# Head of a decoder block kernel: input rows loaded first and handled chunk by chunk, first weight unit in pieces, identity built on the chip, sixteen unread transposes while the rows load

## The chip, the cores and the metric

The kernel runs on one core of a Trainium2 chip. The metric is the device time of one execution in microseconds (us); lower is better. The core has TensorE (PE, with its weight loads PEld), VectorE (DVE), ScalarE (ACT), GpSimd (POOL) and SyncE (SP), which run apart from each other and meet at semaphores.

## The reference

One decoder block on 512 tokens of width 1024, in float32, cut to what matters here:

```python
def rms_norm(x, g):
    y = x * rsqrt(mean(x * x, axis=-1, keepdims=True) + 1e-5)
    return y * g

h = rms_norm(x, norm_mix_g)
proj = h @ w_in                                  # 1024 x 3584: rq, rk, rv, rg, aq, ak, av
rq, rk, aq, ak = (rotary(t, pos) for t in (rq, rk, aq, ak))
ret = silu(rg) * head_group_norm(retention_chunkwise(rq, rk, rv))
att = dilated_mixture(aq, ak, av)
x = x + concat([ret, att], -1) @ w_out
x = x + moe_ffn(rms_norm(x, norm_ffn_g), ...)    # top 4 of 32 experts, each 1024 -> 2x1024 -> 1024
out = rms_norm(x, norm_final_g)
```

## The kernel before

Tokens are cut into four chunks of 128 rows (`NC`). Weights come in units of 1 MB, 128 partitions by 2048 columns, through four buffers `raw`. A float32 product is made of three products in a faster format: ScalarE rounds a unit or an input to its high part (`hi(n)` writes `whi`, `hT_hi` for the input), VectorE subtracts to get the low part (`lo(n)` writes `wlo`, `hT_lo`), and TensorE adds high x high, low x high and high x low. A unit that goes by one of `hi(n)` and `lo(n)` is read by four calls of `unit_chunk`, one for each chunk, with 12 matmuls of 512 columns each.

The head of the kernel, up to the projection's first products, is what the change rewrites. SyncE loads unit 0, then the four row chunks of x, then units 1 to 3. ScalarE's queue loads the gain of the norm and the identity matrix (64 KB of constants), later the other constants and the cosines (`mix`). TensorE waits for the identity, turns the gain, transposes the rows for feature blocks j = 0 to 6 over all four chunks, and ScalarE and VectorE split a feature block of all 512 tokens at a time with the gain as a scale. The row factor 1/rms is not in these inputs: ScalarE squares the four chunks (L790) after `hi(1)`, takes a root (L793), VectorE makes `row_rms` (L1126 to L1130) and multiplies the cosines and sines with it (L1151).

The projection is a list of steps b = 0, 1, 2, ... (`project(b)`): unit n = b // 4, chunk c = b % 4; units 0 and 1 make the first group (AQ), 2 and 3 the next. All engines have the same order of steps written out by hand, and each of them works strictly in its own order. VectorE's order around the head is:

```python
            for b in range(8 * NG):
                n, c = divmod(b, NC)
                gi, u = divmod(n, 2)
                if c == 0 and not 20 <= b < 44:
                    lo(n + 2)
...
                if u == 1 and GROUPS[gi] in (AQ, AK, RQ, RK):
                    rotate(n_rot, b)
```

So `lo(2)`, `lo(3)` and then `rotate(0)` stand behind the scaling of the cosines. TensorE transposes the first rotated rows (`transpose_rot(0)`, L1658) right after step b = 6, and step 7 stands behind it.

Of the kernel before, what the change touches and what calls it, by code (L numbers as in the profile page):

```python
# [25 lines left out]
P = 128  # L26
# [39 lines left out]
LAST_BANK = [0, 2, 6, 4]  # L66

# [88 lines left out]
def build(nc, x, norm_mix_g, w_in, w_out, norm_ffn_g, w_router, b_router,  # L156
# [161 lines left out]
    def sem(name):  # L318
        return nc.alloc_semaphore(name)
# [3 lines left out]
    hi_done, lo_done = sem("hi_done"), sem("lo_done")  # L323
    used = sem("units_used")
# [3 lines left out]
    slots_in, pairs_tok, ones_s = sem("slots_in"), sem("pair_tokens"), sem("ones_ready")  # L328
    has_s, pair_tr, idx_first_s = sem("slots_of_expert"), sem("first_rows_product"), sem("first_rows_index")
    table_cleared, entry_tok, entry_s, entry_out, tab_in = (sem("table_cleared"), sem("entry_tokens"), sem("entries_ready"),  # L330
# [45 lines left out]
    f_sum, f_sq, f_var, f_root, f_out, stored = (sem("final_sum"), sem("final_squares"), sem("final_variance"),  # L376
                                         sem("final_root"), sem("final_rows"), sem("outputs_stored"))
# [23 lines left out]
    HEAD_BANK = [4, 5, 6, 7, 1, 2, 3, 4]  # L401
# [37 lines left out]
    def raw_unit(r, rows):  # L439
        return raw_slot(r).rearrange("p (k c) -> p k c", k=rows)  # L440
# [15 lines left out]
    with block as block:  # L456
        @block.sync
        def _(sp):
# [26 lines left out]
            load(0, 0, mixer_source(0), KU)  # L485
            for c in range(NC):
                sp.dma_start(x1[:, c, :], x[0, c * P:(c + 1) * P, :]).then_inc(x_in[c], 16)
# [61 lines left out]
        def _(pl):  # L549
# [20 lines left out]

            pl.wait_ge(a_prob, NC * H)
# [6 lines left out]
            with nc.allow_non_contiguous_dma(reason="rows of 128 bytes, and 1024 gains onto partitions"):  # L578
# [6 lines left out]
            pl.wait_ge(cst_in, 32)  # L585
# [5 lines left out]
                                  cst[:, C_ROW:C_ROW + NC].unsqueeze(2).to_broadcast([P, NC, TOPK])).then_inc(entry_tok, 1)  # L591
            nc.gpsimd.tensor_copy(tab[:, E, 0:1].bitcast(U32), cst[:, C_OFF:C_OFF + 1])
            nc.gpsimd.tensor_copy(pairs[:, :, :, 0], cst[:, C_TOK:C_TOK + NC].unsqueeze(2).to_broadcast([P, NC, E])
                                  ).then_inc(pairs_tok, 1)
            pl.wait_ge(pairs_tok, 1)
# [140 lines left out]
        def _(act_e):  # L736
# [35 lines left out]
            act_e.dma_start(cst[:, 0:P], small_d[:, 0:P]).then_inc(cst_in, 16)  # L772
            hi(0)
            act_e.wait_ge(gmix_in, GAIN_TURNED)
            nc.scalar.activation(gmix[:, :], ps[:, 0, 0:KD], ACT.Copy).then_inc(gmix_in, 1)
            act_e.wait_ge(cst_in, 16)
            act_e.wait_ge(x_in[NC - 2], 16)
            act_e.dma_start(cst[:, P:C_SMALL], small_d[:, P:C_SMALL]).then_inc(cst_in, 16)
            act_e.dma_start(mix[:, :], mix_d).then_inc(mix_in, 16)
            act_e.dma_start(slot_table, empty_d).then_inc(table_cleared, 16)  # L780
            act_e.wait_ge(gmix_in, GAIN_READY)
            for j in range(KD):
                act_e.wait_ge(xT_tr, j + 1)
                nc.scalar.activation(hT_hi[:, j, :], ps[:, HEAD_BANK[j], :], ACT.Copy,
                                     scale=gmix[:, j:j + 1]).then_inc(hThi_s, 1)
            hi(1)

            for c in range(NC):
                act_e.wait_ge(x_in[c], 16)
                nc.scalar.activation(squares0[:, c, :], x1[:, c, :], ACT.Square,  # L790
                                     accum_out=small[:, 0, c:c + 1]).then_inc(sq, 1)
# [8 lines left out]
            act_e.wait_ge(cst_in, 32)  # L800
# [264 lines left out]
            def final_square(c):  # L1065

                act_e.wait_ge(f_sum, c + 1)
                nc.scalar.activation((y, lin, sig, square_out)[c][:, :], x1[:, c, :], ACT.Square,
                                     accum_out=small[:, 10, c:c + 1]).then_inc(f_sq, 1)
# [8 lines left out]
            for c in range(NC):  # L1078
                final_square(c)
            act_e.wait_ge(f_sq, NC)  # L1080
            nc.scalar.activation(small[:, 12, 0:NC], small[:, 10, 0:NC], ACT.Sqrt, scale=1.0 / D,
                                 bias=cst[:, C_EPS:C_EPS + 1]).then_inc(f_root, 1)
# [4 lines left out]
        def _(v):  # L1087
# [44 lines left out]
            lo(0)  # L1132
            v.wait_ge(gmix_in, GAIN_READY)
            for j in range(KD):
                v.wait_ge(hThi_s, j + 1)
                nc.vector.scalar_tensor_tensor(out=hT_lo[:, j, :], in0=ps[:, HEAD_BANK[j], :], scalar=gmix[:, j:j + 1],
                                               in1=hT_hi[:, j, :].bitcast(F32), op0=ALU.mult,
                                               op1=ALU.subtract).then_inc(hTlo_s, 1)
            lo(1)
# [8 lines left out]
            v.wait_ge(cst_in, 32)  # L1148
# [242 lines left out]
            v.wait_ge(entry_tok, 1)  # L1391
# [7 lines left out]
            v.wait_ge(pairs_tok, 1)  # L1399
# [151 lines left out]
            v.wait_ge(f_sq, NC)  # L1551
            half_var, root, step, rstd = (small[:, k, 0:NC] for k in (11, 12, 13, 3))
            nc.vector.tensor_scalar(half_var, small[:, 10, 0:NC], -0.5 / D, -0.5 * EPS, ALU.mult, ALU.add).then_inc(f_var, 1)
            v.wait_ge(f_var, 1)
            v.wait_ge(f_root, 1)
# [10 lines left out]
        def _(pe):  # L1566
# [31 lines left out]
            pe.wait_ge(cst_in, 16)  # L1598
# [517 lines left out]
```

## Time and profile before

| | before |
|---|---|
| median of 3 runs | 1418.93 us (1418.82 to 1420.3) |
| span of the profiled execution, first to last instruction | 1416.6 us |
| PE busy in the span | 1389.3 us (98%) |
| DVE busy | 1246.5 us (88%) |
| ACT busy | 1055.2 us (74%) |
| POOL busy | 402.8 us (28%) |
| DMA, mean over the span | 320 GB/s |

The profiled execution has a span of 1416.6 us; the median of the runs is 2.3 us above it, which is the time around the first and the last instruction together with what differs between executions. No other time of the profiled execution is listed. Busy time of an engine is the time in which one of its instructions is in flight. Matmuls are pipelined, so one that is shown as 0.39 us long can be followed by the next after 0.23 us.

### The profile page before, as it was taken

Reading aid. Unit: us, or ns where it says so; the run is one execution under the profiler, and the core shown is the slowest. Engines: PE = TensorE matmul, PEld = TensorE weight load, DVE = VectorE, ACT = ScalarE, POOL = GpSimd, SP = SyncE. Lnnn points to the kernel's source line nnn. Section 1 sums busy time; section 2 is a strip of 40 time slices with the busy share of each in tenths; the row PEclk is TensorE's granted clock in tenths of the full one; section 3 lists DMA queues with packets and bytes.
Section 4 is the critical chain, followed back from the end, with each engine's and each line's share of the span. In section 5 each row is a group of like instructions: output and inputs, shape, how many; then the busy total and the mean of one; then the engine's idle time right before and its main releaser. Section 6 shows DMA issues by size and latency. Waiting matters only on the chain.

```text
span 1416.6 us, 19760 instructions
## 1 busy us (share of the span) xinstructions
PE 1389.3 (98%) x6583; PEld 1154.8 (82%) x6583; DVE 1246.5 (88%) x959; ACT 1055.2 (74%) x779; POOL 402.8 (28%) x233
## 2 busy tenths in 40 slices
PE   7999999999999999999999999999999999999996
PEld 6877888878888888888888888888888888888884
DVE  5534647499999999999999999999999999999996
ACT  5234334488888888888888888888888888888875
POOL 0000001067433333333333333333333333333332
PEclk9999999999999999999999999999999999999998
DMA  8311423389999999999999999999999999999993
GB/s 312 106 38 60 134 75 123 124 305 367 385 388 383 382 380 383 379 380 374 380 378 384 375 382 381 380 378 383 382 379 382 383 387 381 383 383 381 383 358 131
DMA packets 80135, 453.73 MB, mean 320 GB/s; under 512 B 12825, under 2 KB 13089, under 8 KB 31852
## 3 DMA queue, kind: packets, MB, share of 16 engines
q1 hardware_dynamic: 68968, 432.55, 77.5%
q0 software_dynamic: 10016, 17.44, 4.8%
q10 hardware_dynamic: 1124, 3.38, 0.7%
q8 instruction: 17, 0.28, 0.1%
q14 instruction: 10, 0.08, 0.0%
HBM read 447.60 MB, written 22.59 MB: 332 GB/s over the span
## 4 chain that ended last, share of the span: by engine, by line
PE 93%; DVE 4%; ACT 2%; DMA 1%; issue 1%; DVEq 0%; ACTq 0%
PE ps L1947 16%; PE ps L1952 16%; PE ps L1948 16%; PE ps L1905 8%; PE ps L1907 8%; PE ps L1913 8%; PE ps L1583 4%; PE ps L1584 4%; PE ps L1591 4%; PE ps L1896 2%; PE ps L1883 2%; DVE wlo L1103 1%; PE ps L1686 1%; DVE wlo L1112 1%; PE ps L1717 1%; PE ps L1667 1%
## 5 line engine op out<-in xcount | busy, mean ns | idle before, releaser
L1947 PE MATMUL ps<-whi,xT_hi 128*128 128x512 f32 x992 | 389.4, 393 | 1.7 <-ACT ps L959 1.0
L1948 PE MATMUL ps<-whi,xT_lo 128*128 128x512 f32 x992 | 386.1, 389 | 0.0
L1112 DVE TENSOR_TENSOR wlo<-raw,whi 128x2048 fp32r<-128x2048 f32 x138 | 315.9, 2293 | 45.6 <-ACT whi L752 45.3
L752 ACT ACTIVATE whi<-raw 128x2048 fp32r<-128x2048 f32 x138 | 264.9, 1920 | 90.2 <-PE ps L1952 71.3
L1108 DVE SCALAR_TENSOR_TENSOR wlo<-raw,gffn,whi 128x2048 fp32r<-128x2048 f32 x124 | 311.0, 2551 | 0.9
L1952 PE MATMUL ps<-wlo,xT_hi 128*128 128x512 f32 x992 | 265.6, 389 | 0.0
L750 ACT ACTIVATE whi<-raw,gffn 128x2048 fp32r<-128x2048 f32 x124 | 245.5, 2004 | 9.9 <-PE ps L1952 9.9
L1947 PEld LDWEIGHTS ps<-whi,xT_hi 128*128 128x128 f32 x992 | 186.4, 188 | 40.6 <-ACT ps L959 1.4
L1952 PEld LDWEIGHTS ps<-wlo,xT_hi 128*128 128x128 f32 x992 | 186.2, 188 | 38.6
L1948 PEld LDWEIGHTS ps<-whi,xT_lo 128*128 128x128 f32 x992 | 186.4, 188 | 37.7
L1905 PE MATMUL ps<-whi,actT_hi 128*128 128x512 f32 x496 | 195.9, 395 | 0.0
L1907 PE MATMUL ps<-whi,actT_lo 128*128 128x512 f32 x496 | 193.2, 390 | 0.0
L1108 DVE SCALAR_TENSOR_TENSOR wlo<-raw_b,gffn,whi 128x2048 fp32r<-128x2048 f32 x62 | 147.1, 2373 | 0.0
L1108 DVE SCALAR_TENSOR_TENSOR wlo<-raw_a,gffn,whi 128x2048 fp32r<-128x2048 f32 x62 | 145.2, 2342 | 0.0
L750 ACT ACTIVATE whi<-raw_a,gffn 128x2048 fp32r<-128x2048 f32 x62 | 124.6, 2010 | 22.0 <-PE ps L1952 22.0
L750 ACT ACTIVATE whi<-raw_b,gffn 128x2048 fp32r<-128x2048 f32 x62 | 124.5, 2008 | 21.9 <-PE ps L1952 21.9
L1913 PE MATMUL ps<-wlo,actT_hi 128*128 128x512 f32 x496 | 132.7, 389 | 0.0
L627 POOL COPY idx_scatter<-tab 128x1 uint32 (+1 forms) x31 | 50.6, 1632 | 286.1 <-ACT y L940 286.0
L627 POOL COPY idx_gather<-tab 128x1 uint32 (+1 forms) x30 | 13.5, 449 | 336.6 <-PE ps L1883 334.2
L1913 PEld LDWEIGHTS ps<-wlo,actT_hi 128*128 128x128 f32 x496 | 93.1, 188 | 19.7
L1907 PEld LDWEIGHTS ps<-whi,actT_lo 128*128 128x128 f32 x496 | 93.2, 188 | 18.4
L1905 PEld LDWEIGHTS ps<-whi,actT_hi 128*128 128x128 f32 x496 | 93.2, 188 | 18.3
(269 smaller groups left out, 1926.2 us busy)
## 6 DMA issues: line engine op xcount, KB each, us to landing
raw<-in_w_gate_up SPq DMA_DIRECT2D x130, 1024.0 KB, 8.6
raw<-in_w_down SPq DMA_DIRECT2D x126, 1024.0 KB, 9.1
raw_a<-in_w_gate_up SPq DMA_DIRECT2D x63, 1024.0 KB, 7.5
raw_b<-in_w_gate_up SPq DMA_DIRECT2D x63, 1024.0 KB, 8.0
raw<-in_w_in SPq DMA_DIRECT2D x14, 1024.0 KB, 5.2
raw<-in_w_out SPq DMA_DIRECT2D x4, 1024.0 KB, 5.0
x<-in_x SPq DMA_DIRECT2D x4, 512.0 KB, 7.4
acc_rows<-x SPq DMA_DIRECT2D x4, 512.0 KB, 5.3
```

The costliest lines, as they stand in the source:

```text
L627: return nc.gpsimd.tensor_copy(index[:, 0:1], tab[:, bass.ds(e, 1), 0].bitcast(U32))
L750: nc.scalar.activation(whi_slot(n), raw_slot(slot_of(n)), ACT.Copy, scale=gffn_of(n)).then_inc(hi_done, 1)
L752: nc.scalar.activation(whi_slot(n), raw_slot(slot_of(n)), ACT.Copy).then_inc(hi_done, 1)
L1108: nc.vector.scalar_tensor_tensor(out=wlo_slot(n), in0=raw_slot(slot_of(n)), scalar=gffn_of(n), in1=whi_slot(n).bitcast(F32), op0=ALU.mult, ...
L1112: nc.vector.tensor_tensor(wlo_slot(n), raw_slot(slot_of(n)), whi_slot(n).bitcast(F32), ALU.subtract).then_inc(lo_done, 1)
L1583: mm(out_ap, x_hi_of(k), w_hi_ap, start=opened and k == 0, stop=False)
L1905: mm(ps[:, bank + half, :], x_hi_t[:, k0 + k, :], w_hi_ap, start=k0 + k == 0 and not started, stop=False, skip_group_check=started)
L1907: mm(ps[:, bank + half, :], x_lo_t[:, k0 + k, :], w_hi_ap, start=False, stop=False, skip_group_check=started)
L1913: last = mm(ps[:, bank + half, :], x_hi_t[:, k0 + k, :], w_lo_ap, start=False, stop=k0 + k == KD - 1, skip_group_check=started)
L1947: mm(ps[:, part, :], xT_hi[:, u, :], w_hi_ap, start=False, stop=False, skip_group_check=True)
L1948: mm(ps[:, part, :], xT_lo[:, u, :], w_hi_ap, start=False, stop=False, skip_group_check=True)
L1952: last = mm(ps[:, part, :], xT_hi[:, u, :], w_lo_ap, start=False, stop=u == U_GU - 1, skip_group_check=True)
```

## The change

SyncE loads x's first chunk, then unit 0 in two halves, then the other chunks. GpSimd builds the identity (a memset of `probT` and an `affine_select`), and TensorE does 16 transposes of it into a bank that nobody reads before it turns the gain. Of the input's eight feature blocks, four (`KU`) are transposed chunk by chunk (`early_input`), chunk c + 1 in the middle of step c; the other four (`late_input`) are transposed for all chunks at the beginning of step 3. Unit 0 is split in four pieces on ScalarE and VectorE, each with a semaphore count of its own. On ScalarE `hi(1)` stands between the chunks 2 and 3, on VectorE `lo(1)` likewise, and the squares stand behind the late feature blocks. Some semaphores are merged (`rows_s` for `entry_tok` and `pairs_tok`; `sq`, `var_s`, `root_s` for the final ones), which leaves every wait at the same place.

```diff
 NOVER = 15
 LAST_BANK = [0, 2, 6, 4]
+WARM = 16
...
+    first_half_in, first_hi, first_lo = sem("first_unit_half_in"), sem("first_unit_hi"), sem("first_unit_lo")
+    ident_s = sem("identity_built")
...
-    HEAD_BANK = [4, 5, 6, 7, 1, 2, 3, 4]
+    EARLY = NC * KU
...
-            for c in range(NC):
+            sp.dma_start(x1[:, 0, :], x[0, 0:P, :]).then_inc(x_in[0], 16)
+            for half, landed in ((0, first_half_in), (1, raw_full[0])):
+                sp.dma_start(raw_unit(0, KU)[:, 2 * half:2 * half + 2, :],
+                             mixer_source(0)[:, 2 * half:2 * half + 2, :]).then_inc(landed, 16)
+            for c in range(1, NC):
                 sp.dma_start(x1[:, c, :], x[0, c * P:(c + 1) * P, :]).then_inc(x_in[c], 16)
...
+            nc.gpsimd.memset(probT[:, :], 0.0).then_inc(ident_s, 1)
+            pl.wait_ge(ident_s, 1)
+            nc.gpsimd.affine_select(out=ident, in_=probT[:, 0:P], pattern=[[-1, P]], compare_op=ALU.not_equal, fill=1.0,
+                                    base=0, channel_multiplier=1).then_inc(ident_s, 1)
...
             act_e.dma_start(gain_rows[0:KD, :], norm_mix_g[0].rearrange("(k p) -> k p", p=P)).then_inc(gmix_in, 16)
-            act_e.dma_start(cst[:, 0:P], small_d[:, 0:P]).then_inc(cst_in, 16)
-            hi(0)
             act_e.wait_ge(gmix_in, GAIN_TURNED)
             nc.scalar.activation(gmix[:, :], ps[:, 0, 0:KD], ACT.Copy).then_inc(gmix_in, 1)
-            act_e.wait_ge(cst_in, 16)
+            act_e.wait_ge(gmix_in, GAIN_READY)
+
+            def input_hi(c):
+
+                for j in range(KU):
+                    act_e.wait_ge(xT_tr, c * KU + j + 1)
+                    nc.scalar.activation(hT_hi[:, j, c * P:(c + 1) * P], ps[:, 4 + j, c * P:(c + 1) * P], ACT.Copy,
+                                         scale=gmix[:, j:j + 1]).then_inc(hThi_s, 1)
+
+            def input_square(c):
+
+                act_e.wait_ge(x_in[c], 16)
+                nc.scalar.activation(squares0[:, c, :], x1[:, c, :], ACT.Square,
+                                     accum_out=small[:, 0, c:c + 1]).then_inc(sq, 1)
+
+            input_hi(0)
+            for k in range(KU):
+                act_e.wait_ge(first_half_in if k < 2 else raw_full[0], 16)
+                piece = slice(k * UW, (k + 1) * UW)
+                nc.scalar.activation(whi_slot(0)[:, piece], raw_slot(0)[:, piece],
+                                     ACT.Copy).then_inc(first_hi if k < KU - 1 else hi_done, 1)
+            input_hi(1)
             act_e.wait_ge(x_in[NC - 2], 16)
             act_e.dma_start(cst[:, P:C_SMALL], small_d[:, P:C_SMALL]).then_inc(cst_in, 16)
             act_e.dma_start(mix[:, :], mix_d).then_inc(mix_in, 16)
+            input_hi(2)
             act_e.dma_start(slot_table, empty_d).then_inc(table_cleared, 16)
-            act_e.wait_ge(gmix_in, GAIN_READY)
-            for j in range(KD):
-                act_e.wait_ge(xT_tr, j + 1)
-                nc.scalar.activation(hT_hi[:, j, :], ps[:, HEAD_BANK[j], :], ACT.Copy,
-                                     scale=gmix[:, j:j + 1]).then_inc(hThi_s, 1)
             hi(1)
-
+            input_hi(3)
+            for j in range(KU, KD):
+                act_e.wait_ge(xT_tr, EARLY + j - KU + 1)
+                nc.scalar.activation(hT_hi[:, j, :], ps[:, j, :], ACT.Copy, scale=gmix[:, j:j + 1]).then_inc(hThi_s, 1)
             for c in range(NC):
-                act_e.wait_ge(x_in[c], 16)
-                nc.scalar.activation(squares0[:, c, :], x1[:, c, :], ACT.Square,
-                                     accum_out=small[:, 0, c:c + 1]).then_inc(sq, 1)
+                input_square(c)
...
-            lo(0)
             v.wait_ge(gmix_in, GAIN_READY)
-            for j in range(KD):
-                v.wait_ge(hThi_s, j + 1)
-                nc.vector.scalar_tensor_tensor(out=hT_lo[:, j, :], in0=ps[:, HEAD_BANK[j], :], scalar=gmix[:, j:j + 1],
+
+            def input_lo(c):
+
+                for j in range(KU):
+                    v.wait_ge(hThi_s, c * KU + j + 1)
+                    rows = slice(c * P, (c + 1) * P)
+                    nc.vector.scalar_tensor_tensor(out=hT_lo[:, j, rows], in0=ps[:, 4 + j, c * P:(c + 1) * P],
+                                                   scalar=gmix[:, j:j + 1], in1=hT_hi[:, j, rows].bitcast(F32),
+                                                   op0=ALU.mult, op1=ALU.subtract).then_inc(hTlo_s, 1)
+
+            input_lo(0)
+            for k in range(KU):
+                v.wait_ge(*((first_hi, k + 1) if k < KU - 1 else (hi_done, 1)))
+                piece = slice(k * UW, (k + 1) * UW)
+                nc.vector.tensor_tensor(wlo_slot(0)[:, piece], raw_slot(0)[:, piece], whi_slot(0)[:, piece].bitcast(F32),
+                                        ALU.subtract).then_inc(first_lo if k < KU - 1 else lo_done, 1)
+            input_lo(1)
+            input_lo(2)
+            lo(1)
+            input_lo(3)
+            for j in range(KU, KD):
+                v.wait_ge(hThi_s, EARLY + j - KU + 1)
+                nc.vector.scalar_tensor_tensor(out=hT_lo[:, j, :], in0=ps[:, j, :], scalar=gmix[:, j:j + 1],
                                                in1=hT_hi[:, j, :].bitcast(F32), op0=ALU.mult,
                                                op1=ALU.subtract).then_inc(hTlo_s, 1)
-            lo(1)
...
-            def unit_chunk(n, out_ap, x_hi_of, x_lo_of, first, opened, closed, ready=None, between=None):
-
-                if first:
+            def unit_chunk(n, out_ap, x_hi_of, x_lo_of, first, opened, closed, ready=None, between=None, by_piece=False):
+
+                if first and not by_piece:
                     hi_ready(n)
                 for k in range(KU):
                     if ready:
                         ready(k)
+                    if by_piece:
+                        pe.wait_ge(*((first_hi, k + 1) if k < KU - 1 else (hi_done, 1)))
                     w_hi_ap, _ = unit_part(n, k)
                     mm(out_ap, x_hi_of(k), w_hi_ap, start=opened and k == 0, stop=False)
                     mm(out_ap, x_lo_of(k), w_hi_ap, start=False, stop=False)
                 if between:
                     between()
-                if first:
+                if first and not by_piece:
                     lo_ready(n)
                 for k in range(KU):
+                    if by_piece:
+                        pe.wait_ge(*((first_lo, k + 1) if k < KU - 1 else (lo_done, 1)))
                     _, w_lo_ap = unit_part(n, k)
                     last = mm(out_ap, x_hi_of(k), w_lo_ap, start=False, stop=closed and k == KU - 1)
                 return last
...
                 return whi_slot(n)[:, k * UW:(k + 1) * UW], wlo_slot(n)[:, k * UW:(k + 1) * UW]
-            pe.wait_ge(cst_in, 16)
+            pe.wait_ge(ident_s, 2)
+            for _ in range(WARM):
+                nc.tensor.transpose(ps[:, 1, 0:P], ident, ident)
             pe.wait_ge(gmix_in, GAIN_IN)
             nc.tensor.transpose(ps[:, 0, 0:KD], gain_rows[0:KD, :], ident[0:KD, 0:KD]).then_inc(gmix_in, 1)
-            def transpose_input(j, c):
-
-                tr = nc.tensor.transpose(ps[:, HEAD_BANK[j], c * P:(c + 1) * P], x1[:, c, j * P:(j + 1) * P], ident)
-                if c == NC - 1:
-                    tr.then_inc(xT_tr, 1)
-
-            for c in range(NC):
+            def early_input(c):
+
                 pe.wait_ge(x_in[c], 16)
-                for j in range(KD - 1):
-                    transpose_input(j, c)
-
-            def last_input():
-
-                pe.wait_ge(hTlo_s, 1)
+                for j in range(KU):
+                    nc.tensor.transpose(ps[:, 4 + j, c * P:(c + 1) * P], x1[:, c, j * P:(j + 1) * P],
+                                        ident).then_inc(xT_tr, 1)
+
+            def late_input(j):
+
                 for c in range(NC):
-                    transpose_input(KD - 1, c)
+                    last = nc.tensor.transpose(ps[:, j, c * P:(c + 1) * P], x1[:, c, j * P:(j + 1) * P], ident)
+                last.then_inc(xT_tr, 1)
+
+            early_input(0)
             drains = []
             for g in GROUPS:
...
                 if b == 0:
                     pe.wait_ge(gmix_in, GAIN_READY)
                 elif b < NC:
-                    pe.wait_ge(hTlo_s, KU + b)
-                elif b == NC:
-                    pe.wait_ge(hTlo_s, KD)
+                    pe.wait_ge(hTlo_s, b * KU + KU)
+                if b == NC - 1:
+                    for j in range(KU, KD):
+                        late_input(j)
                 if u == 0 and gi:
                     s, first = drains[gi - 1]
                     pe.wait_ge(s, first + c + 1)
                 last = unit_chunk(n, ps[:, c, :], lambda k: hT_hi[:, KU * u + k, c * P:(c + 1) * P],
                                   lambda k: hT_lo[:, KU * u + k, c * P:(c + 1) * P], c == 0, u == 0, u == 1,
-                                  ready=(lambda k: pe.wait_ge(hTlo_s, k + 1)) if b == 0 else None,
-                                  between=last_input if b == 0 else (lambda: transpose_cat(H - 1)) if b == 8 * NG - 1 else None)
+                                  ready=((lambda k: pe.wait_ge(hTlo_s, k + 1)) if b == 0 else
+                                         (lambda k: pe.wait_ge(hTlo_s, EARLY + k + 1)) if b == NC else None),
+                                  between=(lambda: early_input(b + 1)) if b < NC - 1 else (lambda: transpose_cat(H - 1)) if b == 8 * NG - 1 else None,
+                                  by_piece=b == 0)
```

## Rows read from the trace of the kernel before

**Rows 1.** The chain that ended last, in order of time: start, length, what

```profile
1.41 6.41 DMA cst<-const_small
...
8.12 4.61 PE ps L1604 x22
...
13.62 0.76 DVE hT_lo L1136
14.52 0.47 PE ps L1583
...
26.67 0.23 PE ps L1583
```

**Rows 2.** Timeline of the queues and of ScalarE, 0 to 20 us

```profile
1.25 2.31 SPq L487 DMA_DIRECT2D x<-in_x  x4
...
3.60 7.00 SPq L467 DMA_DIRECT2D raw<-in_w_in  x4
5.97 1.91 ACT L752 ACTIVATE whi<-raw 128x2048 fp32r<-128x2048 f32 x1 [2.88 <-DMA raw<-in_w_in]
...
8.16 0.18 ACT L775 ACTIVATE gmix<-ps 128x8 f32<-128x8 f32 x1 [0.28 <-PE ps L1600]
...
11.04 0.58 ACTq L780 DMA_DIRECT2D slot_table<-const_empty  x1
```

**Rows 3.** DMA issues of 1.25 us and 3.60 us: KB, us from issue to landing

```profile
x<-in_x SPq DMA_DIRECT2D x1, 512.0 KB, 6.2
...
raw<-in_w_in SPq DMA_DIRECT2D x1, 1024.0 KB, 10.4
```

**Rows 4.** Timeline of TensorE in its transposes, near 8.5 and near 12.7 us

```profile
8.32 0.63 PE L1604 MATMUL ps<-cst,x 128*128 128x128 f32 x2
8.53 0.64 PE L1604 MATMUL ps<-cst,x 128*128 128x128 f32 x2
...
12.56 0.60 PE L1604 MATMUL ps<-cst,x 128*128 128x128 f32 x4
12.67 0.60 PE L1604 MATMUL ps<-cst,x 128*128 128x128 f32 x4
```

**Rows 5.** Groups of GpSimd by line: busy us, mean ns of one

```profile
L694 POOL TENSOR_TENSOR halves<-prod 128x256 f32<-128x256 f32 x1 | 2.7, 2662 | 0.1
...
L597 POOL MEMSET xg<- 128x1024 f32 x1 | 1.0, 952 | 2.8 <-PE ps L1800 2.8
...
L593 POOL COPY pairs<-cst 128x128 f32<-128x128 f32 x1 | 0.4, 422 | 0.0
```

**Rows 6.** Lines that read PSUM or write a split part: ns min/median/max

```profile
L784 ACT ACTIVATE hT_hi<-ps,gmix x8: 682/696/723, 12.8 to 17.6; 128x512 fp32r<-128x512 f32 x8
...
L812 ACT ACTIVATE cat_att<-ps,small x16: 353/358/365, 90.9 to 152.5; 128x128 f32<-128x128 f32 x16
...
L1136 DVE SCALAR_TENSOR_TENSOR hT_lo<-ps,gmix,hT_hi x8: 741/742/751, 13.6 to 18.3; 128x512 fp32r<-128x512 f32 x8
```

**Rows 7.** Timeline of ScalarE and VectorE, 19 to 36 us

```profile
20.01 1.05 ACT L790 ACTIVATE squares<-x 128x1024 f32<-128x1024 f32 x1
...
24.29 1.28 ACT L793 ACT_TABLE_LOAD   x1
...
25.69 3.71 ACT L752 ACTIVATE whi<-raw 128x2048 fp32r<-128x2048 f32 x2
...
28.26 4.49 DVE L1112 TENSOR_TENSOR wlo<-raw,whi 128x2048 fp32r<-128x2048 f32 x2
```

**Rows 8.** Timeline of TensorE's weight loads at step 6's end

```profile
34.80 0.42 PEld L1658 LDWEIGHTS ps<-cst,rot 128*128 128x128 f32 x4 [0.39 <-DVE rot L1172]
```

**Rows 9.** Stretches with granted clock: window, length, busy by engine, PEclk, DMA share, GB/s

```profile
275.00:276.00 1.00, 1.00 (x4) 0.77 (x4) 0.86 (x5) 0.11 (x1) 0.00 (x0) 0.56 0.11 45
...
1403.00:1405.00 2.00, 1.67 (x8) 1.05 (x6) 1.81 (x3) 1.88 (x5) 2.00 (x2) 1.00 0.07 25
...
1407.00:1409.00 2.00, 0.00 (x0) 0.00 (x0) 1.41 (x6) 1.00 (x4) 0.12 (x1) 0.84 0.00 0
```

More of the change, by code:

```diff
@@ L327, in build @@
     GAIN_IN, GAIN_TURNED, GAIN_READY = 16, 17, 18
-    slots_in, pairs_tok, ones_s = sem("slots_in"), sem("pair_tokens"), sem("ones_ready")
+    slots_in, rows_s, ones_s = sem("slots_in"), sem("entry_then_pair_rows"), sem("ones_ready")
     has_s, pair_tr, idx_first_s = sem("slots_of_expert"), sem("first_rows_product"), sem("first_rows_index")
-    table_cleared, entry_tok, entry_s, entry_out, tab_in = (sem("table_cleared"), sem("entry_tokens"), sem("entries_ready"),
+    table_cleared, entry_s, entry_out, tab_in = (sem("table_cleared"), sem("entries_ready"),
                                                             sem("entries_stored"), sem("table_in"))
@@ L375, in build @@
                                           sem("last_rows_summed"))
-    f_sum, f_sq, f_var, f_root, f_out, stored = (sem("final_sum"), sem("final_squares"), sem("final_variance"),
-                                         sem("final_root"), sem("final_rows"), sem("outputs_stored"))
+    f_sum, f_out, stored = sem("final_sum"), sem("final_rows"), sem("outputs_stored")
+    SQ_FINAL, VAR_FINAL, ROOT_FINAL = 3 * NC, NC + 1, NC + 1
     v_full = [sem(f"over_raw_full{r}") for r in range(RAW)]
@@ L483, in load_bias_rows @@
                 sp.dma_start(row_l[0:1, :], b_gate_up[0, bass.ds(i + e, 1), D:2 * D]).then_inc(bias_in, 16)
-            load(0, 0, mixer_source(0), KU)
-            for c in range(NC):
+            sp.dma_start(x1[:, 0, :], x[0, 0:P, :]).then_inc(x_in[0], 16)
[3 more added lines that the diff above has]
+            for c in range(1, NC):
                 sp.dma_start(x1[:, c, :], x[0, c * P:(c + 1) * P, :]).then_inc(x_in[c], 16)
@@ L583, in _ @@
             nc.gpsimd.partition_broadcast(br[:, :], br_row[0:1, :]).then_inc(br_s, 1)
-            pl.wait_ge(cst_in, 32)
+            pl.wait_ge(cst_in, 16)
             nc.gpsimd.tensor_copy(tri_r[:, :], cst[:, C_TRI:C_TRI + P]).then_inc(ones_s, 1)
@@ L590, in _ @@
             nc.gpsimd.tensor_copy(entry[:, :, 0].bitcast(U32).rearrange("p (c k) -> p c k", c=NC),
-                                  cst[:, C_ROW:C_ROW + NC].unsqueeze(2).to_broadcast([P, NC, TOPK])).then_inc(entry_tok, 1)
+                                  cst[:, C_ROW:C_ROW + NC].unsqueeze(2).to_broadcast([P, NC, TOPK])).then_inc(rows_s, 1)
             nc.gpsimd.tensor_copy(tab[:, E, 0:1].bitcast(U32), cst[:, C_OFF:C_OFF + 1])
             nc.gpsimd.tensor_copy(pairs[:, :, :, 0], cst[:, C_TOK:C_TOK + NC].unsqueeze(2).to_broadcast([P, NC, E])
-                                  ).then_inc(pairs_tok, 1)
-            pl.wait_ge(pairs_tok, 1)
+                                  ).then_inc(rows_s, 1)
+            pl.wait_ge(rows_s, 2)
             pl.wait_ge(logit_s, NC)
@@ L798, in cat_hi @@
                 nc.scalar.activation(cat_part(q)[0], ps[:, 4 + q % H, :], ACT.Copy).then_inc(c_hi, 1)
-            act_e.wait_ge(cst_in, 32)
+            act_e.wait_ge(cst_in, 16)
             copied = {AV: avt, RG: rgt, RV: rvt}
@@ L1068, in final_square @@
                 nc.scalar.activation((y, lin, sig, square_out)[c][:, :], x1[:, c, :], ACT.Square,
-                                     accum_out=small[:, 10, c:c + 1]).then_inc(f_sq, 1)
+                                     accum_out=small[:, 10, c:c + 1]).then_inc(sq, 1)
             def final_scale(c):
@@ L1079, in _ @@
                 final_square(c)
-            act_e.wait_ge(f_sq, NC)
+            act_e.wait_ge(sq, SQ_FINAL + NC)
             nc.scalar.activation(small[:, 12, 0:NC], small[:, 10, 0:NC], ACT.Sqrt, scale=1.0 / D,
-                                 bias=cst[:, C_EPS:C_EPS + 1]).then_inc(f_root, 1)
+                                 bias=cst[:, C_EPS:C_EPS + 1]).then_inc(root_s, 1)
             final_scale(0)
@@ L1147, in _ @@
             v.wait_ge(mix_in, 16)
-            v.wait_ge(cst_in, 32)
+            v.wait_ge(cst_in, 16)
             angles = mix[:, M_COS:M_COS + 2 * NC * DH].rearrange("p (s c d) -> p s c d", s=2, c=NC)
@@ L1390, in _ @@
             shares = entry[:, :, 1].rearrange("p (c k) -> p c k", c=NC)
-            v.wait_ge(entry_tok, 1)
+            v.wait_ge(rows_s, 1)
             link(nc.vector.tensor_tensor(shares, gates[:, :, :], small[:, 2, 0:NC].unsqueeze(2).to_broadcast([P, NC, TOPK]),
@@ L1398, in _ @@
             nc.vector.tensor_copy(counts[:, :], ps[:, 5, NC * E:NC * E + E]).then_inc(counts_s, 1)
-            v.wait_ge(pairs_tok, 1)
+            v.wait_ge(rows_s, 2)
             link(nc.vector.tensor_copy(pairs[:, :, :, 3], pair_pos[:, :, :]))
@@ L1550, in _ @@
                 final_sum(c)
-            v.wait_ge(f_sq, NC)
+            v.wait_ge(sq, SQ_FINAL + NC)
             half_var, root, step, rstd = (small[:, k, 0:NC] for k in (11, 12, 13, 3))
-            nc.vector.tensor_scalar(half_var, small[:, 10, 0:NC], -0.5 / D, -0.5 * EPS, ALU.mult, ALU.add).then_inc(f_var, 1)
-            v.wait_ge(f_var, 1)
-            v.wait_ge(f_root, 1)
+            nc.vector.tensor_scalar(half_var, small[:, 10, 0:NC], -0.5 / D, -0.5 * EPS, ALU.mult, ALU.add).then_inc(var_s, 1)
+            v.wait_ge(var_s, VAR_FINAL + 1)
+            v.wait_ge(root_s, ROOT_FINAL + 1)
             link(nc.vector.reciprocal(root, root))
```

## Prediction, made blind

> **What bounds the kernel now.** I read the page's busy shares first, then the chain of waits, the timeline of each engine over the first 36 us, the landing times of the DMAs, and stretches with the granted clock. TensorE is busy 1389.3 of 1416.6 us. Of the 27 us that are missing, 7.86 us pass before its first instruction, 1.14 us before the first product, and 11.9 us after its last work near 1404.7 [rows 9]. It stands still for about 6 us in all in between. So the kernel is TensorE's list of work, and time that the head wins or loses is carried to the end, unless another engine's chain holds TensorE up.
>
> The head goes: identity issued at 1.41 and here at 7.82 us, transposes from 8.05 on, first split block at 14.37, first product at 14.52, step 4 at 26.67 [rows 1] (the chain counts a matmul to its end; by starts it is 26.51). A step is 12 products at 0.2275 us, 2.73 us, so TensorE has step 6 behind it at 34.7. Then comes the row to remember: the transposes of the first rotated rows start at 34.80, the weight load having waited 0.39 us for VectorE [rows 8]. VectorE's chain to that point has no slack at all: squares end at 24.27, table load for the root at 24.29, cosines scaled, `lo(2)` and `lo(3)` without a gap from 28.26, then `rotate(0)` [rows 7]. It takes 10.5 us from the end of the squares to TensorE's transposes (34.8 - 24.3). So two things must come earlier for the kernel to be faster: TensorE's first product, and the end of the squares. A head that helps only the first helps nothing.
>
> **The change, part by part.**
>
> *Rows first.* Unit 0 (1 MB) was released at 5.97, x's first chunk, half a MB behind it, at 1.25 + 6.2 = 7.45, unit 1 at 3.60 + 10.4 = 14.0 [rows 2, 3]. From 7.45 to 14.0 the queue brought 2.5 MB, 1.31 us for each half. It is a queue in order, so in the new order the chunks land like this: chunk 0 at 5.97 - 1.3 = 4.7, the halves of unit 0 at 6.0 and 7.3, chunks 1 to 3 at 8.6, 9.9 and 11.2, unit 1 at 13.85 (64 KB of identity less, 0.16 us). One more issue on SyncE (7.00 us for four, most of it waiting for room; 0.58 us each for x) makes the later ones half a us later. The data in front of them hides it; without that cover it would cost 0.5 us.
>
> *Identity.* A memset of 128x512 and a select of 128x128 on GpSimd. The trace has no select. From below, a copy of 128x128 costs 0.42 us; from above, the dearest elementwise row, 128x256 with two inputs, 2.66 us; the memset is half of 0.95 us [rows 5]. The select reads one input, so I take 0.9, near the copy. From 0.8 us on, with two handovers: ready at 2.3 us; the ends are 1.8 and 4.1.
>
> *Sixteen transposes.* At 8.3 us transposes start every 0.213 us, at 12.6 every 0.11 [rows 4]: the lower level, 1.2 GHz, and then 2.4 GHz, after 4.3 us of transposes from 7.86 (the granted-clock column says 1.00 throughout; the spacing tells more). 16 x 0.213 = 3.4, so the gain is turned at 5.75, 1.05 us after chunk 0 is there. They are queued in front of real work: ScalarE's gain (0.30 us later, 0.18 long) and everything behind it wait for them. In return I take the clock to be at 2.4 GHz for the first product.
> The Trainium skill says otherwise ("TensorE: Matmul & The Clock Gate", Part 4: transposes do not count as activity the way matmuls do, and full clock does not engage for them). The trace disagrees: the spacing halved with transposes alone on the engine. By that rule step 0 would run at 1.2 GHz, and the sum would be some 2.4 us longer.
>
> *Chunk 0 and unit 0.* A 128x128 split costs ScalarE 0.36 us (L812, same shape, same kind of scale); 128x512 ones of 0.70 follow each other at 0.58, so these at 0.24. VectorE's 128x512 takes 0.74; for a quarter of it I take 0.34, one each 0.28 [rows 6]. Transposes of chunk 0 start at 5.95 and end at 7.06; the four high parts of the input end at 7.5; unit 0's pieces, a quarter of 1.91 us and a start, take 0.6 and follow at 0.5, so the first is ready at 8.04 and the last at 9.54. First product 8.1, 6.4 us earlier than before. Step 0: products of the fourth piece until 10.05, four transposes of chunk 1 (0.44), four low products (0.91): end 11.4. VectorE's low pieces, 0.63 each, are done at 10.7 and hold up nothing.
>
> *Chunks 1 and 2.* From the first transpose of a chunk to its last low part: 0.31 + 0.36 + 0.05 + three times 0.28 + 0.34 = 1.9 us. TensorE fills 1.35 of these with transposes and low products. So each later step waits about 0.55 us. Step 1 starts at 11.96, step 2 at 15.70.
>
> *Chunk 3, and what stands ahead of it.* ScalarE has chunk 2 ready at 15.07, issues the table's DMA (0.58, [rows 2]) and does `hi(1)` 15.67 to 17.58. VectorE does `lo(1)` (2.25) until 19.85 and only then chunk 3's low parts, done at 21.0. TensorE transposed chunk 3 at 17.5, ended step 2 at 18.87, and waits 2.2 us. Queued behind it: the 16 late transposes (1.76 us) and step 3. Step 4 starts at 21.04 + 1.76 + 2.73 = 25.5, 1.0 us earlier than before: of 6.4 us, 2.6 went to 24 more transposes inside the steps and 3.3 to these waits; half a us came back, since step 0 has fewer gaps.
>
> *Late blocks, then squares.* The first late block is transposed 0.64 us after 21.04; ScalarE does four at 0.58: until 24.0. Now the squares, 4.26 us as before: 28.27. Before: 24.27. They stood directly behind `hi(1)`; now two more blocks of work stand in between. The chain of 10.5 us follows, and TensorE can transpose rotated rows at 38.8 instead of 34.8. It reaches that point at 25.5 + 8.2 = 33.7 and stands for 5.0 us; step 7 and everything after it are 4.0 us late.
>
> *The clock after the stop.* The longest stop before was the head's. At the end TensorE's work stops near 1404.7 and the clock falls inside 1407 to 1409 (0.84 of two us: 0.64 us at half, so at 1408.4), and in the thin work before 275 it fell, too, without a real stop [rows 9]. After 5.0 us I expect it low. What that costs is between nothing and half the 4.3 us that it took to rise in the head: 2.1. I take 1.9.
>
> Sum: +4.0 + 1.9 = 5.9 us. Against the profiled span 1416.6 -> 1422.5; against the median 1418.93 -> 1424.8. Merged semaphores and the move of constants on ScalarE's queue cost nothing: their waits are met long before (0.9 us of issues at 11.9 lie in ScalarE's idle time ahead of chunk 2, and would cost that much in the chain if chunk 2 came sooner).
>
> **Rivals.**
> 1. The same stop with the clock still high, or a shorter one. The chain can't be much shorter: even with the identity for nothing, unit 1 lands at 13.85, so `hi(1)` ends at 15.8, `lo(1)` at 18.1, chunk 3 at 19.2, late blocks at 22.2, squares at 26.5: +2.2. So +2.2 to +4.0, 1421.1 to 1422.9. For it: clock falls are rare in this trace. Against: 5 us is longer than the 3.7 us after which it fell at the end.
> 2. A dearer head. Each us by which the identity is later moves everything by one (to +1.8); step 0 at 1.2 GHz takes twice its 12 products and four transposes (8.1 + 3.6 + 0.85 + 1.8 = 14.4, where step 1 had 11.96) and adds 2.4; late transposes at 1.2 GHz after the 2.2 us wait add 1.3, as 0.85 us for each block is then longer than ScalarE's 0.58. With one or two of them: +7 to +10, 1426 to 1429. By the trace one of the three is quite possible.
> 3. Other side: VectorE's chain gives way. It decides if the squares end before 33.7 - 10.5 = 23.2 us, or if the 10.5 us are shorter than in the trace. Then step 4's gain counts: -1.0, 1417.9, and without the wait for `lo(1)` as well -3.2, 1415.7. For it: TensorE went on only 0.1 us after its own work, so the limit is seen only once and barely. Against: VectorE had no idle time between 28.26 and the rotation, and its order is not changed.
>
> **How the numbers follow.** My case 0.48, rival 1 0.20, rival 2 0.22, rival 3 0.10. A measurement of this kernel can tell about 0.2%, 2.8 us, from no change. Slower by more: my case, rival 2 and most of rival 1, 0.82. Within: the short end of rival 1 and most of rival 3, 0.14. Faster: 0.04. The range leaves out rival 3 and the far end of rival 2: 1420.8 to 1428.6. My case alone: 1423 to 1426.5.
>
> **What would show it.** First product near 8.1; `hi(1)` ahead of chunk 3 and a wait of TensorE for `hT_lo` near 19 to 21; squares ending near 28; a wait of some 5 us for `rot` with the granted clock at 0.5 behind it; step 4 about 1 us earlier but step 7 about 4 us later. Wrong if the squares end by 25, if TensorE doesn't wait at L1658's first transposes, or if the first product comes after 10.

## The result, and the profile after

The changed kernel takes 1424.64 us (median of 4 runs, 1424.30 to 1426.43) against 1419.01 us (median of 4, 1418.82 to 1420.30): ratio 1.0042, 95% interval 1.0028 to 1.0056. It is 5.6 us slower, 0.4%, and the interval lies clear of 1. A later comparison on another chip gave 1.0052 (1.0037 to 1.0067).

The page of the changed kernel, its span and its busy times:

```profile
span 1423.0 us, 19828 instructions
...
PE 1392.7 (98%) x6599; PEld 1156.8 (81%) x6599; DVE 1248.3 (88%) x974; ACT 1056.6 (74%) x794; POOL 401.4 (28%) x235
```

The timeline of the changed kernel's head, all engines (start, length, engine, line):

```profile
1.78 0.29 POOL L579 TENSOR_SCALAR_AFFINE_SELECT cst<-probT 128x128 f32<-128x128 f32 x1 [0.50 <-POOL probT L577]
...
2.13 3.67 PE L1648 MATMUL ps<-cst 128*128 128x128 f32 x16 [2.13 <-POOL cst L579]
...
5.94 0.94 PE L1656 MATMUL ps<-cst,x 128*128 128x128 f32 x4
...
7.53 2.20 ACT L803 ACTIVATE whi<-raw 128x512 fp32r<-128x512 f32 x4
...
8.31 0.47 PE L1629 MATMUL ps<-whi,hT_hi 128*128 128x512 f32 x1 [1.44 <-ACT whi L803]
...
12.31 0.50 PE L1629 MATMUL ps<-whi,hT_hi 128*128 128x512 f32 x1 [0.36 <-DVE hT_lo L1165]
...
15.58 1.93 ACT L762 ACTIVATE whi<-raw 128x2048 fp32r<-128x2048 f32 x1
...
17.54 2.29 DVE L1138 TENSOR_TENSOR wlo<-raw,whi 128x2048 fp32r<-128x2048 f32 x1 [1.45 <-ACT whi L762]
...
18.10 0.60 PE L1656 MATMUL ps<-cst,x 128*128 128x128 f32 x4
...
19.75 1.12 DVE L1165 SCALAR_TENSOR_TENSOR hT_lo<-ps,gmix,hT_hi 128x128 fp32r<-128x128 f32 x4
...
20.92 1.97 PE L1662 MATMUL ps<-cst,x 128*128 128x128 f32 x16 [1.29 <-DVE hT_lo L1165]
...
25.49 0.39 PE L1629 MATMUL ps<-whi,hT_hi 128*128 128x512 f32 x1
```

The identity is ready at 2.1 us, the first product starts at 8.31 instead of 14.52 [rows 1], and TensorE has that lead of 6.2 us in hand. Then the lead shrinks. Steps 1 and 2 wait for the low parts of chunks 1 and 2. From 17.54 to 19.83 VectorE is busy with `lo(1)`, while chunk 3, whose transposes started at 18.10, lies waiting for it. The late transposes (L1662) start at 20.92. Step 4 starts at 25.49 against 26.51 before, so 1.0 us of the lead is left.

The timeline of ScalarE and VectorE of the changed kernel, 19 to 50 us, answers to [rows 7]:

```profile
23.91 1.07 ACT L796 ACTIVATE squares<-x 128x1024 f32<-128x1024 f32 x1
...
27.98 0.20 ACT L796 ACTIVATION_READ_ACCUMULATOR squares<-x 128x1 f32 x1
28.20 1.28 ACT L819 ACT_TABLE_LOAD   x1
...
29.61 3.71 ACT L762 ACTIVATE whi<-raw 128x2048 fp32r<-128x2048 f32 x2
...
32.16 4.49 DVE L1138 TENSOR_TENSOR wlo<-raw,whi 128x2048 fp32r<-128x2048 f32 x2
...
37.95 0.69 DVE L1216 TENSOR_TENSOR rot<-rot,rtmp 128x512 f32<-128x512 f32 x1
```

TensorE at the same place, 32 to 42 us, answers to [rows 8]:

```profile
32.75 1.07 PE L1639 MATMUL ps<-wlo,hT_hi 128*128 128x512 f32 x4
38.70 1.12 PE L1709 MATMUL ps<-cst,rot 128*128 128x128 f32 x4 [4.88 <-DVE rot L1216]
...
40.47 0.63 PE L1629 MATMUL ps<-whi,hT_hi 128*128 128x512 f32 x1
40.90 0.63 PE L1630 MATMUL ps<-whi,hT_lo 128*128 128x512 f32 x1
```

Each row of ScalarE and VectorE stands 3.9 us later than its partner of before: squares end 28.18 for 24.27, table load 28.20 for 24.29, `lo(2)` 32.16 for 28.26. TensorE is through with step 6 a microsecond early and then stands for 4.88 us. Behind the stop its products start 0.43 us apart (40.47, 40.90) instead of 0.23: it runs at 1.2 GHz. The granted clock (PEclk, the third number from the end) in stretches of 2 us says the same:

```profile
36.00:38.00 2.00, 0.00 (x0) 0.00 (x0) 1.97 (x5) 0.00 (x0) 0.00 (x0) 0.82 0.91 325
38.00:40.00 2.00, 1.30 (x5) 1.25 (x6) 1.97 (x4) 0.15 (x1) 0.00 (x0) 0.50 1.04 403
...
44.00:46.00 2.00, 2.00 (x12) 1.69 (x11) 0.81 (x2) 0.91 (x2) 0.00 (x0) 0.97 0.00 0
```

It fell at 37.3 us (0.82 of two us: 0.72 us at half), 3.5 us after TensorE's last work ended at 33.82, and rose again at 44.1 (0.97 of two us: 0.12 us at half).

Where the 6.4 us of the two spans lie, by the starts of the same TensorE instructions in both traces:

```
                                                   before    after    later by
first transposes of rotated rows                    34.80    38.70      3.90
fifth group of them                                 58.52    64.96      6.44
first product that reads actT_hi                   340.2    345.6       5.4
last product that reads actT_hi                   1384.3   1389.8       5.5
end of the span                                   1416.6   1423.0       6.4
```

3.9 us come with the stop (4.88 us long, reached 1.0 us early), 2.54 with the low clock behind it. 1.0 is given back before 340 us: the trace of before has 3.4 us at 1.2 GHz from 275 on, worth at most 1.7, which this one has not (it waits 0.8 us more for `whi` near 320). The last 1.0 us comes in TensorE's final stretch. There it waits 1.5 us for nothing that the profile shows, behind the branch around the overflow loop, whose body does not run. Before it waited 0.3 us there.

### The profile page after: what moved, and what is told of

Its sections match the earlier page's. It is cut to its first block, busy times and chain, and to the rows that moved or that the text cites. A ratio compares the mean times of both kernels' runs of the same rounds, so it can differ in the third digit from the quotient of the medians.

```text
span 1423.0 us, 19828 instructions
## 1 busy us (share of the span) xinstructions
PE 1392.7 (98%) x6599; PEld 1156.8 (81%) x6599; DVE 1248.3 (88%) x974; ACT 1056.6 (74%) x794; POOL 401.4 (28%) x235
## 4 chain that ended last, share of the span: by engine, by line
PE 91%; DVE 4%; ACT 2%; issue 1%; DMA 1%; DVEq 0%; POOL 0%; ACTq 0%; POOLq 0%
PE ps L1998 16%; PE ps L2003 16%; PE ps L1999 16%; PE ps L1956 8%; PE ps L1958 8%; PE ps L1964 8%; PE ps L1629 4%; PE ps L1630 4%; PE ps L1639 4%; PE ps L1947 2%; PE ps L1934 2%; DVE wlo L1138 1%; DVE wlo L1129 1%; PE ps L1737 1%; PE ps L1768 1%
```

## The experiments

In each, the numbers of the head are from its one profiled execution. The times of all kernels have a spread of some us.

**1. The squares in idle time (e1_squares_early).** Of the changed kernel only the place of the four squares on ScalarE is different. Squares 0 to 2 go into time in which ScalarE was idle.

```diff
+            input_square(0)
             input_hi(1)
...
+            input_square(1)
+            input_square(2)
             input_hi(2)
...
             input_hi(3)
+            input_square(3)
...
-            for c in range(NC):
-                input_square(c)
```

> Theory (VectorE's chain from the squares to the first rotation stops TensorE for 4.9 us, and the clock falls in that stop): squares in ScalarE's idle time end near 21.6 us instead of 28.2. The root's first VectorE step then waits for the late low parts (25.1), and the rotation ends near 34.5 instead of 38.6. TensorE's stop at the first rotated rows shrinks from 4.9 to about 0.9 us, the clock stays high there, and the time is about 1418.7 us (the theory allows 1417 to 1420.5). Rival (the time is lost in the waits of steps 1 to 3 and in the 24 more transposes, the stop only shows it): the time stays above 1422.

Measured: ratio to before 1.0014 (1.0004 to 1.0024), median 1420.59 us (10 runs, 1417.70 to 1423.79) against 1418.17. TensorE in its profile, 34 to 36 us:

```profile
34.56 0.66 PE L1711 MATMUL ps<-cst,rot 128*128 128x128 f32 x4 [0.76 <-DVE rot L1218]
```

The stop is 0.76 us, the clock stays at 1.00, and the first rotated rows are transposed 0.2 us earlier than before. The squares end 7.6 us earlier than in the changed kernel (20.59 for 28.18), but the rotated rows come only 4.1 us earlier, since VectorE makes the late low parts until 25.1 and starts with the root behind them. The last product that reads `actT_hi` starts at 1383.2, 6.6 us earlier than in the changed kernel. So up to there, four instructions of 1.04 us each, moved on an engine that is 74% busy, take back all of the loss: the kernel before is at 1384.3 there, with its 3.4 us at 1.2 GHz. The time as a whole is above the 1418.7 forecast, and just above the 1420.5 that the theory allowed: 2.4 us of the 5.6 remain against before. In this profile TensorE waited 2.6 us behind the final branch, and 3.4 us at 1.2 GHz fell into the same stretch. Whether the other nine executions lose their time there too isn't shown.

**2. `lo(1)` behind chunk 3 (e2_lo1_behind_chunk3).**

```diff
-            lo(1)
             input_lo(3)
+            lo(1)
```

> VectorE does the low parts of chunk 3 ahead of lo(1). Theory: late transposes start near 19.95 instead of 20.92 us, everything behind them, the squares too, is 1.0 us earlier, the stop stays at 4.9 us: about 1423.6. Rival (only the head's own waits count, the stop does not): the 1.0 us is won at step 3 and nothing changes in the end, or the stop grows by it: 1424.6.

Measured: 1426.16 us (4 runs, 1424.85 to 1431.05), ratio to before 1.0062 (1.0042 to 1.0082); first rotated rows at 38.53, stop 4.9 us. Neither number came: the late transposes started at 20.75, 0.17 us earlier, not 1.0. TensorE's wait for chunk 3 did fall from 1.3 to 0.4 us, but the clock went low inside step 0, as its timeline shows:

```profile
5.92 0.66 PE L1656 MATMUL ps<-cst,x 128*128 128x128 f32 x4
...
9.22 0.69 PE L1629 MATMUL ps<-whi,hT_hi 128*128 128x512 f32 x1
9.71 0.63 PE L1630 MATMUL ps<-whi,hT_lo 128*128 128x512 f32 x1
10.13 0.63 PE L1629 MATMUL ps<-whi,hT_hi 128*128 128x512 f32 x1
```

Steps 0 and 1 lost most of what step 3 won. The edit stands behind both steps, so it did not make the clock fall there. What the edit is worth by itself stays open from this run. That the stop is as long as ever agrees with the theory.

**3. No unread transposes (e3_no_warm).** `WARM = 0` in the changed kernel.

> No transposes of the identity. Theory (they buy the full clock for step 0): first product near 7.3 us instead of 8.3, but step 0 runs in good part at 1.2 GHz; step 1 starts between 12.0 and 13.5 us instead of 12.3, and the time is 1424.3 to 1425.8. Rival (they only delay real work): step 1 starts near 11.3, and the time is 1423.6.

Measured: 1425.90 us (4 runs, 1424.02 to 1426.64), ratio to before 1.0045 (1.0029 to 1.0062). TensorE from 1 to 8 us:

```profile
2.28 0.24 PE L1650 MATMUL ps<-cst,gain_rows 8*128 8x8 f32 x1 [2.28 <-DMA gain_rows<-in_norm_mix_g]
4.16 1.11 PE L1656 MATMUL ps<-cst,x 128*128 128x128 f32 x4 [1.64 <-DMA x<-in_x]
6.54 0.77 PE L1629 MATMUL ps<-whi,hT_hi 128*128 128x512 f32 x1 [1.26 <-ACT whi L803]
7.10 0.63 PE L1630 MATMUL ps<-whi,hT_lo 128*128 128x512 f32 x1
7.53 0.63 PE L1629 MATMUL ps<-whi,hT_hi 128*128 128x512 f32 x1
```

The first product starts 1.8 us earlier, but at 1.2 GHz: the products are 0.43 us apart (7.10, 7.53). ScalarE also waits until 8.2 us for the second half of unit 0. Step 1 starts at 12.55 instead of 12.31. So the transposes delay real work by 1.8 us and give 2.0 back, in part as clock; in these two profiles they win 0.24 us. The median is 0.1 us above the range that the theory gave, and times that spread by 2 us and more can't tell the two kernels apart.

**4. The stop filled with unread transposes (e4_fill_stop, s4_fill_stop_again).** Nothing of the work is moved; TensorE only has something to do while it waits.

```diff
             def transpose_rot(q):

+                for _ in range(44 if q == 0 else 0):
+                    nc.tensor.transpose(ps[:, 7, 0:P], ident, ident)
                 pe.wait_ge(rot_s, q + 1)
```

> 44 transposes of the identity with unread results fill TensorE's stop ahead of the first rotated rows (4.8 us at 0.11 us each); nothing else changes. Theory (the low clock behind the stop costs 2.7 us): the granted clock stays at 2.4 GHz behind 38.7 us and the time is about 1421.9. Rival (the low clock is hidden behind other waits): 1424.6.

> The kernel of e4 (44 unread transposes in the stop), in more rounds, since its four times went from 1421.7 to 1427.7. Theory (the low clock behind the stop costs 2.5 us in every run): the profile has no low clock before 64 us again, and the mean of the times is 2 to 3 us below that of the changed kernel on the same chip. Rival (it fell by chance, or falls elsewhere instead): no more than 1 us below.

Measured: 1425.34 us (4 runs, 1421.70 to 1427.70), and again 1424.26 us (6 runs, 1422.04 to 1426.82), beside the changed kernel on the same chip at 1424.96 (6 runs, 1424.28 to 1428.70). The ratios to before there are 1.0038 (1.0024 to 1.0052) and 1.0052 (1.0037 to 1.0067). TensorE in the first profile, and two stretches with the granted clock:

```profile
33.66 4.97 PE L1704 MATMUL ps<-cst 128*128 128x128 f32 x44
38.71 0.65 PE L1711 MATMUL ps<-cst,rot 128*128 128x128 f32 x4
...
39.67 0.39 PE L1629 MATMUL ps<-whi,hT_hi 128*128 128x512 f32 x1
39.91 0.39 PE L1630 MATMUL ps<-whi,hT_lo 128*128 128x512 f32 x1
```

```profile
36.00:38.00 2.00, 2.00 (x21) 2.00 (x19) 1.97 (x5) 0.00 (x0) 0.00 (x0) 1.00 0.92 336
38.00:40.00 2.00, 1.92 (x14) 1.55 (x13) 1.97 (x4) 0.60 (x1) 0.00 (x0) 1.00 1.04 387
```

The rotated rows come at 38.71 as before the edit, the clock stays high, and the fifth group of them starts at 62.42 (62.55 in the second profile) instead of 64.96. So inside the stage the low clock costs 2.5 us, in both profiles. At the end of the kernel less is left: the last product that reads `actT_hi` starts 2.2 us earlier than in the changed kernel's profile in the first, 0.8 us in the second, where 3.4 us at 1.2 GHz came at 294 us instead. The times show even less. The first four have their median at 1425.3, where 1421.9 was forecast: by them the rival (1424.6) is nearer. The mean of the six later ones is 1424.4 against 1426.0 beside them, 1.6 us less, between the two forecasts, and the intervals overlap. That the stop lowers the clock is shown; that avoiding it shortens the whole kernel by the same amount is not.

**5. The kernel before, with its squares delayed (f3_before_squares_late).** The same suspicion from the other side.

```diff
             hi(1)
+            hi(2)
...
-                if c == 0 and not 20 <= b < 44:
+                if c == 0 and not 20 <= b < 44 and b:
                     hi(n + 2)
```

> The kernel before with hi(2) ahead of the four squares on ScalarE, nothing else. Theory (the chain from the squares to the first rotation has no slack): squares end 1.8 us later, TensorE transposes the first rotated rows at 36.6 instead of 34.8 us after a stop of 1.9 us, and the time is 1.8 us longer than before (1420 to 1421). Rival (the chain has slack): the same time as before.

Measured: 1421.04 us (10 runs, 1419.49 to 1422.60) against 1418.74, ratio 1.0017 (1.0008 to 1.0027). ScalarE's squares, and TensorE's wait:

```profile
22.10 1.04 ACT L791 ACTIVATE squares<-x 128x1024 f32<-128x1024 f32 x1
```

```profile
36.87 0.66 PE L1659 MATMUL ps<-cst,rot 128*128 128x128 f32 x4 [1.75 <-DVE rot L1173]
```

The squares are 2.1 us late (22.10 for 20.01 in [rows 7]), the rotated rows 2.1 us, the last product that reads `actT_hi` 2.0 us (1386.3 for 1384.3), the median 2.3. The delay is passed on one for one: the chain has no slack. This stop of 1.75 us did not lower the clock.

**6. The root out of the late chain (f1_root_first, f2_root_first_no_warm, s6_root_first_no_warm_again).** The changed head with squares 0 and 3 on VectorE and 1 and 2 on ScalarE, all in idle time, the root ahead of chunk 2, and `lo(1)` behind chunk 3; f2 and s6 are the same kernel with `WARM = 0`. On VectorE:

```diff
+            vector_square(0)
             v.wait_ge(gmix_in, GAIN_READY)
...
+            vector_square(3)
+            v.wait_ge(sq, NC)
+            nc.vector.tensor_scalar(small[:, 1, 0:NC], small[:, 0, 0:NC], 1.0 / D, EPS, ALU.mult, ALU.add).then_inc(var_s, 1)
             input_lo(2)
-            lo(1)
+            v.wait_ge(var_s, 1)
+            v.wait_ge(root_s, 1)
+            inverse_root(small[:, 1, 0:NC], small[:, 2, 0:NC], row_rms[:, :], small[:, 13, 0:NC])
+            v.sem_inc(rstd_s, 1)
             input_lo(3)
+            lo(1)
...
-            v.wait_ge(sq, NC)
...
-            inverse_root(small[:, 1, 0:NC], small[:, 2, 0:NC], row_rms[:, :], small[:, 13, 0:NC])
-            v.sem_inc(rstd_s, 1)
```

> The changed head with the row factor out of VectorE's late chain: squares of chunks 0 and 3 on VectorE, of 1 and 2 on ScalarE, all in idle time; root ahead of chunk 2; lo(1) behind chunk 3. Theory (only TensorE's list of work is left as the limit): no wait for the first rotated rows, transposes of them near 32.7 us instead of 34.8 before, last expert's products 2.1 us earlier than before, time 1416 to 1417 where the rest of the kernel has the same clock. Rival (something else in the head holds TensorE up by as much): first rotated rows at 34.5 or later, time as the kernel before or above.

> The kernel of f1 without the 16 unread transposes. With them left out of the changed kernel, step 1 started at 12.55 instead of 12.31 us. Theory (they are worth 0.2 to 0.3 us): first rotated rows 0.2 to 0.3 us later than in f1, which the times can't tell. Rival (they cost, now that nothing hides the head): at least 0.5 us earlier than in f1.

> The kernel of f2, in more rounds. Its first rotated rows were transposed 1.6 us earlier than before, and 0.7 us of that was left at the last expert. Theory: 0 to 1 us below the kernel before, at the edge of what the times can tell. Rival (the head's gain is not real): equal or slower.

Measured: f1 1419.53 us (11 runs, 1417.57 to 1423.64), ratio to before 1.0009 (1.0000 to 1.0018). Without the unread transposes 1418.42 us (11 runs, 1416.03 to 1420.62), ratio 0.9996 (0.9987 to 1.0005), and again 1417.62 us (12 runs, 1415.32 to 1422.03), ratio 0.9993 (0.9984 to 1.0003). The first rotated rows, in f1, and in the second profile without the unread transposes:

```profile
33.64 0.60 PE L1718 MATMUL ps<-cst,rot 128*128 128x128 f32 x4
```

```profile
32.33 0.60 PE L1718 MATMUL ps<-cst,rot 128*128 128x128 f32 x4
```

No wait stands behind either row: nothing but TensorE's own list holds them. They come 1.2 and 2.5 us earlier than before (33.17 in the profile of f2, 1.6 us earlier), where 2.1 was forecast for f1. In f1 the clock went low at 8.6 us, in the middle of step 0, although 16 transposes had gone ahead, and rose again at 12.0; that goes with its falling short. In the other two profiles the low clock of step 0 ended once, at 11.3 and 9.8 us, and did not come back in the head. So the expectation for f2, 0.2 to 0.3 us later, failed: its rows came 0.5 us earlier than in f1. What the unread transposes cost or win here isn't shown, though. The two profiles of the same kernel without them lie 0.84 us apart, more than that difference, and f1 is the one profile with them. The medians of f1 and f2, 1.1 us apart with ranges of 6 and 4.6 us, fit a cost but do not settle it. Over the whole kernel the gain is 0.4 to 0.7 in a thousand, and both intervals include 1. This version takes back all that the change lost; that it beats the kernel before isn't shown.

**7. A second look at the changed kernel (r1_after_again, s5_changed_timed).**

> A second profile of the changed kernel. Up to the step after the first rotated rows it should repeat the first within 0.2 us (transposes at 38.7, clock low until 44 us). The stretch behind the last expert, where TensorE waited 1.5 us behind a branch and before 0.3, and the place of short stretches of low clock should differ if they are chance, and repeat if the change makes them.

> The changed kernel itself, beside the others on the same chip: 1424 to 1425.5 us, 0.4% above the kernel before.

Measured: 1424.66 us, and 1424.96 us (6 runs). Three profiles in all have the first rotated rows at 38.70, 38.72 and 38.72, the stop at 4.9 us, the low clock from 37.3 to 44.1, the fifth group at 64.96, 64.98 and 64.97. The stop and the fall belong to the change. The wait behind the final branch was, in the waits of TensorE of the first two profiles:

```profile
PE ps L2126 <- issue: 1.5, 1, 1.5
```

```profile
PE ps L2126 <- issue: 1.7, 1, 1.7
```

It is 1.3 us in the third, 2.6 us in e1, absent in both profiles of experiment 4, and 1.8 us in f3, whose TensorE program is that of the kernel before, but 0.3 in the profile of before. So the change does not make it, and 1.2 us of the 6.4 between the two spans lie in a wait that differs by chance. What sets it stays open.

## Why the prediction was right

Forecast 1424.8 us, measured 1424.6: right in its mechanism, a stop of TensorE for VectorE's chain with a low clock behind it. That it is also right to 0.2 us is luck, as the last point below tells. The steps, in their order:

- *Identity at 2.3 us:* 2.1. The select took 0.29 us, less than the lower bound of 0.42 from the copy.
- *Landing times:* chunk 0 was forecast at 4.7 and came by 4.16 (e3 starts on it then), 0.54 us early; the second half of unit 0 was forecast at 7.3, and in e3 ScalarE waits for it until 8.2. Neither is seen in the changed kernel, as both lie behind the 16 transposes and ScalarE's pieces.
- *Sixteen transposes, 3.4 us, then full clock:* the gain was turned at 5.73 (forecast 5.75). The first products are 0.31 and 0.24 us apart, so the clock was high. Of the rule of the Trainium skill that transposes don't bring full clock ("TensorE: Matmul & The Clock Gate", Part 4), the trace shows the opposite here: nothing but transposes stood ahead of 8.31 us. But e2 and f1 show that the level so won can be lost again within step 0.
- *First product 8.1, step 1 at 11.96, step 2 at 15.70:* 8.31, 12.31, 16.15. The 1.9 us from a chunk's first transpose to the next step came out (10.41 to 12.31, 14.26 to 16.15). Too short was what was summed for the eight products ahead of the transposes: 2.10 and 1.95 us, where 1.95 and 1.82 were taken.
- *`hi(1)` at 15.67, `lo(1)` until 19.85, late transposes at 21.04:* 15.58, 19.83, 20.92. Step 2 ended half a microsecond later than forecast, and the wait for chunk 3 took that up.
- *Squares end at 28.27, rotated rows at 38.8, stop of 5.0 us, +4.0:* 28.18, 38.70, 4.88, +3.90. The chain from squares to rotation took 10.5 us, as read off before. Run f3 moves its beginning in the kernel before and moves its end by as much. In e1 the beginning moves further than the end, because VectorE's late low parts then hold the chain up.
- *The clock, +1.9:* mis-sized, +2.54, above even the 2.1 that was given as the upper end. It stayed low for 6.8 us, 5.4 of them under work. The forecast had taken the 4.3 us of the head as the longest.
- *Not forecast:* that the low stretch at 275 us would not be there (-1.0 with the 0.8 us wait behind it), and the longer wait in the tail (+1.0). They cancel. The span grew by 6.4 us where 5.9 was forecast, the median by 5.6: the forecast lies between them, and that the sum came within 0.2 us of the median owes something to both.

Rival 1 (clock stays high, or a shorter stop) is ruled out by three profiles with a stop of 4.9 us and 6.8 us at the low level, rival 2 (a dearer head) by the head's own times, rival 3 (the chain has slack) by f3.

## What to carry to other kernels

Before a head is made faster on the engine that is busy all the time, look for the chain on the other engines that meets it at the first join, and ask how much slack it has: here TensorE already waited 0.1 us for it, and the new order put 3.9 us in front of it. A long stop on TensorE can cost the clock behind it as well: here 3.9 us of delay became 6.4 a few steps later. Small work that a late chain begins with belongs in idle time that exists earlier, even where its own engine has plenty left.

## What the runs showed of the hardware

- After a stop of 4.88 us TensorE's clock was at 1.2 GHz, after stops of 1.75 and 0.76 us at this place it was not. In e1's final stretch it fell inside a wait of 2.6 us. With 44 unread transposes in the stop it stayed at 2.4 GHz (e4, s4).
- Sixteen transposes, 0.213 us apart, were followed by first products at 2.4 GHz in all eight profiles that have them. In six of these the clock stayed high through step 0, in e2 and f1 it went low again at 9.3 and 8.6 us. In the two, the four transposes of chunk 0 took 0.66 us, so the clock was high by then; in the six they took 0.87 to 1.11 us. The waits ahead of the first product were 1.58 us in the two and 1.27 to 1.51 in the six. Why it fell isn't shown.
- A GpSimd select of 128x128 that builds an identity takes 0.29 us, and a memset of 128x512 0.53 us.
- VectorE squares and sums 128x1024 in 1.22 us where ScalarE takes 1.05.
- TensorE's wait behind the branch around the overflow loop, whose body does not run, was between nothing and 2.6 us from profile to profile.
